# One fp32 product per attention step instead of three split ones, and score masks added in PSUM by VectorE

## The reference

```
s_c = q @ k_cmp - slope * d_c          p_c = masked_softmax(s_c, d_c >= 0)           o_c = p_c @ v_cmp
s_s = q @ k_selected - slope * d_s     p_s = masked_softmax(s_s, d_s >= 0)           o_s = p_s @ v_selected
s_w = q @ k_window - slope * d_w       p_w = masked_softmax(s_w, 0 <= d_w < 512)     o_w = p_w @ v_window
out = gate0 * o_c + gate1 * o_s + gate2 * o_w
```

## Time and profile before

| | |
|---|---|
| time, median of 3 runs | 1501.54 us (1500.02 to 1504.7) |
| profiled execution | 1494.26 us, span 1492.6 us |
| PE busy | 1435.1 us, 96% of the span |
| PEld, DVE, ACT, POOL busy | 1140.0, 736.6, 448.3, 123.4 us |
| chain that ended last | PE 87%, DVE 4%, issue 2%, POOL 2%, ACT 2% |
| granted clock of PE, 40 slices | 9999999799997999999999999999999999999998 |
| DMA | 67.61 MB, 45 GB/s over the span |

### The profile page before, as it was taken

One profiled execution on the slowest core, in us unless ns is written; L12 is line 12 of the kernel. 1 busy time (PEld: TensorE's weight loads), 2 busy tenths in 40 slices (PEclk: granted clock), 3 DMA queues, 4 the chain that ended last, 5 costly groups with the idle time before them and its releaser, 6 DMA issues.

```text
span 1492.6 us, 17479 instructions
## 1 busy us (share of the span) xinstructions
PE 1435.1 (96%) x6654; PEld 1140.0 (76%) x6654; DVE 736.6 (49%) x916; ACT 448.3 (30%) x635; POOL 123.4 (8%) x85
## 2 busy tenths in 40 slices
PE   7999999999897998989999999999999999999996
PEld 6788888876565765668888888888888888888884
DVE  6333511496665956655344435344443534444355
ACT  6211201404786047843132121212112121211212
POOL 0011000000111001110001000101000010100013
PEclk9999999799997999999999999999999999999998
DMA  5111120000000030011101111111111111111102
GB/s 207 53 57 56 33 89 33 9 1 4 1 1 6 1 116 1 1 57 57 56 29 57 43 57 57 42 42 56 42 42 56 56 42 42 56 42 42 56 0 112
DMA packets 19837, 67.61 MB, mean 45 GB/s; under 512 B 2216, under 2 KB 2984, under 8 KB 19624
## 3 DMA queue, kind: packets, MB, share of 16 engines
q1 hardware_dynamic: 19548, 66.03, 13.0%
q0 software_dynamic: 240, 0.93, 0.3%
HBM read 63.01 MB, written 4.19 MB: 45 GB/s over the span
## 4 chain that ended last, share of the span: by engine, by line
PE 87%; DVE 4%; issue 2%; POOL 2%; ACT 2%; DMA 1%; SPq 0%; DVEq 0%; POOLq 0%; ACTq 0%
PE PS L321 18%; PE PS L322 18%; PE PS L325 18%; PE PS L1303 5%; PE PS L1300 5%; PE PS L1299 5%; PE PS L1108 3%; PE PS L1109 2%; PE PS L1204 2%; PE PS L1206 1%; PE PS L1205 1%; PE PS L1185 1%; DVE nmax L824 1%; PE PS L1186 1%; PE PS L1090 1%
## 5 line engine op out<-in xcount | busy, mean ns | idle before, releaser
L321 PE MATMUL PS<-R,wh 128*128 128x512 f32 x1200 | 470.3, 392 | 13.1 <-DVE wl L313 11.2
L322 PE MATMUL PS<-R,wh 128*128 128x512 f32 x1200 | 468.2, 390 | 0.0
L325 PE MATMUL PS<-R,wl 128*128 128x512 f32 x1200 | 370.7, 390 | 0.0
L321 PEld LDWEIGHTS PS<-R,wh 128*128 128x128 f32 x1200 | 226.2, 188 | 61.2 <-DVE wl L313 11.7
L325 PEld LDWEIGHTS PS<-R,wl 128*128 128x128 f32 x1200 | 226.0, 188 | 47.3
L322 PEld LDWEIGHTS PS<-R,wh 128*128 128x128 f32 x1200 | 225.9, 188 | 47.4 <-issue 0.7
L306 ACT ACTIVATE wh<-raw 128x1024 fp32r<-128x1024 f32 x97 | 101.9, 1050 | 260.2 <-PE PS L1303 174.0
L961 DVE TENSOR_TENSOR F<-PS,F 128x1024 f32<-128x1024 f32 x80 | 97.8, 1223 | 86.6 <-PE PS L1303 86.6
L876 DVE TENSOR_TENSOR wl<-raw,wh 128x512 fp32r<-128x512 f32 x148 | 102.7, 696 | 59.1 <-ACT raw L605 57.1
L1300 PE MATMUL PS<-R,wh 128*128 128x512 f32 x320 | 124.5, 389 | 0.0
L1299 PE MATMUL PS<-R,wh 128*128 128x512 f32 x320 | 124.5, 389 | 0.0
(11 more groups left out here) (159 smaller groups left out, 1459.6 us busy)
## 6 DMA issues: line engine op xcount, KB each, us to landing
raw<-in_w_units SPq DMA_DIRECT2D x97, 512.0 KB, 3.4
F<-in_xT SPq DMA_DIRECT2D x16, 512.0 KB, 8.5
outT<-F SPq DMA_DIRECT2D x16, 256.0 KB, 2.2
F<-in_w_cmp SPq DMA_DIRECT2D x1, 2048.0 KB, 7.9
masks<-in_masks POOLq DMA_DIRECT2D x1, 448.0 KB, 4.9
R<-in_alibi_q POOLq DMA_DIRECT2D x2, 160.0 KB, 4.5
R<-R SPq DMA_DIRECT2D x4, 48.0 KB
R<-in_alibi_k POOLq DMA_DIRECT2D x1, 136.0 KB, 3.6
```

What stands on the lines that cost most here:

```text
L321: nc.tensor.matmul(out, w_h, hi(kt)[:, cols], start=first, stop=False)
L322: nc.tensor.matmul(out, w_h, lo(kt)[:, cols], start=False, stop=False)
L325: last = nc.tensor.matmul(out, w_l, hi(kt)[:, cols], start=False, stop=end)
```

## The change

- The exponential is taken once, in fp32, into `EB`. `V` is kept unsplit in fp32, in `PBm`. `values(s)` is a single fp32 product, V against `EB[s % 4]`.
- In the second pass the mask is no product any more: DVE adds it to the scores in PSUM (`mask_tile`), two steps ahead of its other work of a step, and ACT waits for it. The masks for the keys' side lie transposed in `masks` (diagonal and edge) and, for the compressed branch, in a new 512 KB table `CM` that POOL's queue loads ahead of the ALiBi rows. The first pass keeps its mask products. NEG becomes -2**100.
- `OT` moves from `PBm` to F1 slots 5 and 6. So SP loads the residual input for k = 2..7 where it did, and k = 0, 1 after the last `turn`. The copy of V ahead of its transposition is gone.
- The loop over the groups is written out on every engine, with constants in the waits.
- Weight units 24 to 26 wait for the last value product instead of the last subtraction, since `EB` lies in `raw`.

```diff
-NEG = -1e30
+NEG = -2.0 ** 100
...
+        def mask_of(s):
+            i, br, j = STEPS[s]
+            if br == 2:
+                return f32(CM[:, i * P:(i + 1) * P])
+            if j == i:
+                return masks[:, M_TILES:M_TILES + P]
+            return masks[:, M_TILES + P:M_TILES + 2 * P] if br == 1 and j == i - WT else None
...
-            with sp.Fori(0, KV) as g:
+            for g in range(KV):
...
-            for k in range(KT):
+            for k in range(2, KT):
                 sp.dma_start(F1[:, X1 + k, :], xT[k]).then_inc(x1_in, 16)
-            sp.wait_ge(pt_lo, KV * NS)
+            sp.wait_ge(pv_done, KV * NS)
             load(sp, 24, 0, 0, 0)
             load(sp, 25, 0, 0, 0)
             load(sp, 26, 0, 0, 0)
+            sp.wait_ge(ot_turned, KV * TT)
+            for k in range(2):
+                sp.dma_start(F1[:, X1 + k, :], xT[k]).then_inc(x1_in, 16)
...
             pool.dma_start(KB[DH:DH + AR + MR, :], alibi_k).then_inc(ak_in, 16)
-            with pool.Fori(0, KV) as g:
+            pool.dma_start(CM, cmp_masks_d).then_inc(cm_in, 16)
+            for g in range(KV):
...
-            with act.Fori(0, KV) as g:
+            for g in range(KV):
...
-                        nc.scalar.activation(PTH[s % 4], PS[:, s % 4, :], ACT.Exp).then_inc(pt_hi, 1)
-                        nc.scalar.activation(EB[s % 4], PS[:, s % 4, :], ACT.Exp).then_inc(e_ready, 1)
+                for s in range(NS):
+                    act.wait_ge(st_ready, NS * g + s + 1)
+                    if mask_of(s) is not None:
+                        act.wait_ge(masked, masked_upto(g, s))
+                    if s > 3:
+                        act.wait_ge(pv_done, NS * g + s - 3)
+                    nc.scalar.activation(EB[s % 4], PS[:, s % 4, :], ACT.Exp).then_inc(e_ready, 1)
+                    later(s)
...
+                def mask_tile(s):
+                    mask = mask_of(s)
+                    if mask is None:
+                        return
+                    dve.wait_ge(st_ready, NS * g + s + 1)
+                    scores = PS[:, s % 4, :].rearrange("p (h q) -> p h q", h=GROUP)
+                    nc.vector.tensor_tensor(scores, scores, mask.rearrange("p (o q) -> p o q", o=1)
+                                            .broadcast_to([P, GROUP, P]), ALU.add).then_inc(masked, 1)
...
+                mask_tile(0)
+                mask_tile(1)
                 for s in range(NS + 6):
-                    if s < NS:
-                        dve.wait_ge(e_ready, NS * g + s + 1)
-                        nc.vector.tensor_tensor(PTL[s % 4], EB[s % 4], f32(PTH[s % 4]), ALU.subtract).then_inc(pt_lo, 1)
+                    if s + 2 < NS:
+                        mask_tile(s + 2)
...
-                    nc.tensor.matmul(out, VH[:, n, 0:DH + 1], PTH[s % 4], start=first, stop=False)
-                    nc.tensor.matmul(out, VL[:, n, 0:DH + 1], PTH[s % 4], start=False, stop=False)
-                    nc.tensor.matmul(out, VH[:, n, 0:DH + 1], PTL[s % 4], start=False, stop=end).then_inc(pv_done, 1)
+                    nc.tensor.matmul(out, V[:, n, 0:DH + 1], EB[s % 4], start=first, stop=end).then_inc(pv_done, 1)
```

More of the change, by code:

```diff
@@ L76 @@
 NCON = 2 * P + TT
[L79 to L80 removed]
+M_ID, M_DIAG, M_EDGE, M_CMP = 0, P, 2 * P, 3 * P
+M_TILES = M_CMP + TT * CW
+NMASK = M_TILES + 2 * P
 class Steps:
@@ L189, in f32, with masked_upto @@
             return ap.bitcast(F32)
+        def mask_of(s):
[5 more added lines that the diff above has]
+            return masks[:, M_TILES + P:M_TILES + 2 * P] if br == 1 and j == i - WT else None
+        def masked_upto(g, s):
+            tiles = [n for n in range(NS) if mask_of(n) is not None]
+            return len(tiles) * g + sum(n <= s for n in tiles)
         consts_in, late_in, w1_in, ak_in = sem("consts_in"), sem("late_in"), sem("w1_in"), sem("ak_in")
-        masks_in, params_in = sem("masks_in"), sem("params_in")
+        masks_in, params_in, cm_in, masked = sem("masks_in"), sem("params_in"), sem("cm_in"), sem("masked")
         g_hi, g_lo, r_ready, conv_ready, tapr_ready = (sem("g_hi"), sem("g_lo"), sem("r_ready"), sem("conv_ready"),
@@ L593, in _, with later @@
                 act.wait_ge(vt_ready, g + 1)
[L594 to L595 removed]
+                nc.scalar.activation(V[:, 0:2 * TT, 0:DH].rearrange("p (b j) d -> p b j d", b=2),
+                                     pair(2).rearrange("p (j b d) -> p b j d", b=2, d=DH), ACT.Copy).then_inc(v_ready, 1)
                 act.wait_ge(kvc_ready, 2 * g + 2)
[L597 to L605 removed]
+                nc.scalar.activation(V[KCMP:KCMP + NCMP, 2 * TT, 0:DH], CMP_OUT[1][0:NCMP, 0:DH], ACT.Copy).then_inc(kc_hi, 1)
+                def later(s):
                     if s - 2 in ENDS and ENDS.index(s - 2) % 3 == 1:
@@ L614, in _ @@
                         act.wait_ge(o_ready, TT * g + i + 1)
-                        nc.scalar.activation(SQ_HEADS, F1[:, bass.ds(Q0 + 2 * g, 2), i * P:(i + 1) * P], ACT.Square,
-                                             accum_out=head_ss[:, bass.ds(TT * g + i, 1)]).then_inc(osq_ready, 1)
+                        nc.scalar.activation(SQ_HEADS, F1[:, Q0 + 2 * g:Q0 + 2 * g + 2, i * P:(i + 1) * P], ACT.Square,
+                                             accum_out=head_ss[:, TT * g + i:TT * g + i + 1]).then_inc(osq_ready, 1)
+                for s in range(NS):
[6 more added lines that the diff above has]
+                    later(s)
+                for s in range(NS, NS + 3):
+                    later(s)
                 act.wait_ge(pv_done, NS * g + NS)
@@ L791, in _ @@
             nc.vector.tensor_copy(posb[:, :], PS[:, 7, BANK // 2:BANK // 2 + 2]).then_inc(posb_ready, 1)
-            with dve.Fori(0, KV) as g:
-                steps.enter(g, KV, 2 * TT)
+            for g in range(KV):
                 for half in range(2):
@@ L885, in _ @@
                             part(STEP_OF_TURN.index(s - later))
-                steps.leave()
             dve.wait_ge(osq_ready, KV * TT)
@@ L1083, in _ @@
             pe.wait_ge(ak_in, 16)
-            pe.wait_ge(clear_ready, 5)
-            with pe.Fori(0, KV) as g:
+            pe.wait_ge(clear_ready, 4)
+            for g in range(KV):
                 def compressed_hidden(kv, src, pairs=range(CMP_BLOCK // 2)):
@@ L1181, in key_scores @@
                     flat = lambda q: q.rearrange("p h q -> p (h q)")
-                    mask = {0: M_DIAG if j == i else None,
-                            1: M_DIAG if j == i else M_EDGE if j == i - WT else None,
-                            2: M_CMP + i * P}[br]
                     nc.tensor.matmul(out, KA[:, cols], flat(QA[:, i, :, :]), start=True, stop=False)
                     last = nc.tensor.matmul(out, KB[0:DH + AR + MR, cols], flat(QB[0:DH + AR + MR, i, :, :]),
-                                            start=False, stop=mask is None)
-                    if mask is not None:
-                        last = nc.tensor.matmul(out, masks[:, mask:mask + P], masks[:, M_ID:M_ID + GROUP * P],
-                                                start=False, stop=True)
+                                            start=False, stop=True)
                     last.then_inc(st_ready, 1)
@@ L1458 @@
     first = lambda a: np.asarray(a)[0].reshape(16, P, P).transpose(1, 0, 2).reshape(P, 2, 1024)
-    consts, masks, aq, ak = _shape_constants()
+    consts, masks, cmp_masks, aq, ak = _shape_constants()
     arrays = {
@@ L1464 @@
         "w_cmp2": A(np.stack([np.asarray(w_ck2)[0], np.asarray(w_cv2)[0]], axis=1)),
-        "params": A(params), "consts": consts, "masks": masks, "alibi_q": A(aq), "alibi_k": ak,
+        "params": A(params), "consts": consts, "masks": masks, "cmp_masks": cmp_masks, "alibi_q": A(aq), "alibi_k": ak,
     }
```

84 lines of the change are left out of this document (33 added, 51 removed).

## The result

| | before | after |
|---|---|---|
| time, median | 1502.72 us (1500.02 to 1504.7, 4 runs) | 1489.21 us (1488.22 to 1493.21, 4 runs) |
| ratio | | 0.9917, 95% interval 0.9899 to 0.9935 |
| profiled execution | 1494.26 us, clock 0.981 | 1493.21 us, clock 0.978 |
| PE busy | 1435.1 us, 96% | 1449.6 us, 97% |
| DVE, ACT busy | 736.6, 448.3 us | 676.1, 381.5 us |

The change makes the kernel 12.5 us faster by the ratio. The two profiled executions say something else again: they differ by 1.05 us. That of before was shorter than each of its four timed runs, that of after the longest of its own. So the first lesson is to ask which execution a profile shows.

A forecast was written before the change was run, and what follows sets the result against it. PE was taken as the bound in the second pass, and its loop jump and lower clock as the cost between groups. Second passes +1.4 us and between groups -5.7 gave -4.3: 1497.2 us from a 1501.54 median, range 1491.5 to 1503.

The forecast's parts named there:

- the last of the sum: Whole kernel: -4.3 us, made against the profiled 1494.26 us, applied to the median 1501.54, 7.28 higher, giving 1497.2.
- Streaming: Second pass on PE: one fp32 product for three adds 24.7 us, masks leaving PE save 12.3; +12.4 us in all.
- Waits: Second pass: PE's waits shrink from 9.5 to 4.0 us per group, bounds 0 and 9.5; with streaming +1.4 us in all.
- 98.2 + 6.2 + 2.5: Second pass per group, us: old streaming with eight turnings, added streaming, and the tail after the last turning that stays.
- Between the groups: From group 0's last scaling to group 1's scores: writing the loop out removes PE's jump; -5.7 us, bounds 0 and -9.
- the first of the two cases: Between the groups: PE's clock falls all the same, near 464.1 us, during the compression; 5.0 us saved.
- a rival: Between the groups: the gap stays, or its gain returns as a wait for the ALiBi rows; 1502.9 us, chance 0.20.
- Edits at nothing: First-pass masks, V copy, mask table, weight units 24 to 26 and residual slots 0 and 1: each counted at 0 us.
- Clock kept, waits gone: Second-pass waits fall to 1.5 us per group and the clock stays up entering group 1: 1492.5 us, chance 0.20.
- Masks late: Second pass: DVE's mask additions sit behind scaling and bank copies, exposing 16 scalings, 15.5 us: 1512.7 us, chance 0.10.

The follow-up runs named there:

- after_again: The changed kernel itself, unchanged, timed and profiled again: 1489.57 us, ratio 0.9931 to the kernel before.
- before_filled: The kernel before plus ten unread matmuls per group where PE waits for the window copy at tile 3: 1497.99 us, ratio 0.9987.
- unroll_only: The kernel before with the loops over the groups written out on every engine, nothing else: 1493.28 us, ratio 0.9954.
- before_held: The kernel before plus unread matmuls in four PE waits per group (ALiBi rows, maxima, last scaling, tile 3): 1489.44 us, ratio 0.9932.
- fill_only_2: The changed kernel plus unread matmuls in three PE waits per group (maxima, last scaling, ALiBi rows): 1484.5 us, ratio 0.9884 to the kernel before.
- The square: Written-out loops, ratios to the kernel before: split products 0.9954 (masks on PE), 1.0076 (on DVE); one fp32 product 0.9976 (PE), 0.9931 (DVE).
- one_product: The changed kernel with its second-pass masks taken back to products on PE, single fp32 product kept: 1498.46 us, ratio 0.9976 to the kernel before.
- split_dve_masks: The kernel before with written-out loops and masks added by DVE, three split products kept: 1513.31 us, ratio 1.0076.
- pe_unrolled: The kernel before with the loop over the groups written out on PE alone: 1497.11 us, ratio 0.9961.
- loops_kept: The changed kernel with the group loops kept as loops and a copy of V ahead of its transposition: 1494.57 us, ratio 0.9964 to the kernel before.
- filled_all: The changed kernel plus earlier ALiBi load for group 1 and unread matmuls in three waits and among group-entry products: 1482.55 us, ratio 0.9878 to before.

## Why the prediction was wrong

**The step that failed** is the last of the sum: "a difference carries over: 1501.54 - 4.3 = 1497.2". The 4.3 us were made against an execution of 1494.26 us, which gave 1490.0. The profile of after_again, with the same entry of group 0 as that one, has 1489.15, so up to here the sum was nearly right. The 7.28 us added after that did not carry over: the changed kernel's median (1489.21) lies on its profile, not 7 us above it. They were the kernel before's own loss. Its profiled execution had a clock of 0.981, its usual one has 0.976 to 0.977; at 1.24 to 1.5 us per 0.001 that is 5 to 7.5 us.

Shown: the time of before follows its clock; matmuls that nobody reads, whose only use is to keep PE busy in its waits, gain 10.6 us in the kernel before and 5 in the changed one; and with these in both kernels the difference falls to 4.9 us (6.6 by the means). Not shown: where the usual execution of before loses more clock than that of after. The wait for the window copy at tile 3 is one such place, with up to 4.0 us per pass, and in the changed kernel it is down to 0.4 us; but with this wait filled before_filled recovered only 2 of the 10.6 us. unroll_only has the wait too, and none of its six runs is above 1494.5 us. The entry of group 0 moves executions by up to 4.6 us in either kernel. Nor is it known what decides in a single execution whether the clock falls behind a wait of 2.5 us.

Point by point, by the prediction's own terms:

- **Streaming, +12.4 us.** Right in its parts: 0.86 us for the fp32 product, 0.23 for a score product, 1.32 per step (0.86 + 2 x 0.23).
- **Waits, 9.5 to 4.0 us per group.** Mis-sized, by 1.3 us per group. With the clock at its upper level in both, the pass is 110.2 us before and 109.6 after [before_held, fill_only_2], -0.6 per group where +0.7 was forecast. 98.2 + 6.2 + 2.5 leave 2.7 us of waits instead of 4.0. In the two groups that is -1.1 instead of +1.4, within its bounds of -6.6 and +12.4. The square shows how: the dearer product, which takes longer than the chain behind it needs, hides the waits it would otherwise meet (110.2 to 115.0 us with masks on PE, 4.8 us for 148 / 2 x 0.167 = 12.4 of streaming), and on top of that the masks' 6.15 us of streaming give 3.6 (115.0 to 111.4), or 5.4 against the pass with fillers (109.6).
- **Between the groups, -5.7 us.** The size was right (-5.6 and -5.1 in the two profiles), the make-up only in part. The gap was PE's jump, 4.0 us. The clock did fall, as in the first of the two cases, which had 5.0 us. In the first profile the bound behind it is the load of the ALiBi rows after POOL's sums, which I had only named in a rival. The gain beyond the gap goes roughly with how long after PE's start the clock falls: 1.9 us in after and 1.8 in one_product (stage of 7.32 and 7.76 us), 1.0 in after_again (7.90), 0.5 in split_dve_masks (8.43), and before the start in unroll_only and pe_unrolled (8.85, as before). What sets that is open. The Trainium skill's rule on sequential prefetch (Runtime: NRT & Kernel Launch, section Instruction fetch mechanics) says that a taken branch to a page that isn't held has to fetch it first. The trace agrees as far as it goes: 0.05 us in straight code, 3.62 to 4.05 with the loop.
- **Edits at nothing.** All held. Everything behind the last scaling takes 841.58 us, against 841.91. PE waits nowhere for the residual input. The mask table delays nothing: in after_again the first score product of group 0 starts at 288.80 us, against 289.67 before.
- **Rivals.** "Clock kept, waits gone" came nearest in time (1492.5) and had 0.20. It was priced by waits at 1.5 us per group and a clock that stays up at the entry of group 1. The waits did go, the clock at the entry did not stay. That the time came out near this rival is luck: about half of the gain is clock that the kernel before loses in executions that no profile shows, and the rival had it elsewhere. "Masks late" was wrong here. Something like it happens in split_dve_masks, where DVE has the subtraction as well: +12 us in the pass of group 0, by waits for the subtraction (10.3 us) and the clock.

## What to carry to other kernels

A profile is one execution. Before a difference is added to a median, compare the mean clock of the profiled execution with the clocks of the timed runs; where they differ, part of the median hangs on the clock, and it need not come back in another kernel. Before two profiles are subtracted, look for a stage ahead of the change that differs between them. Two edits on one path are priced together: here each alone made group 0's second pass longer, by 4.8 us (a product that is dearer but leaves an engine free) and 11.9 (a job given to that engine), and both together by 1.2. PE's waits of 1 to 3 us were worth filling with matmuls that nobody reads into a free bank: 5 us in the changed kernel, 10.6 in the kernel before.

## What the runs showed of the hardware

- The jump back to the head of PE's loop over the groups costs 3.6 to 4.1 us (loops_kept 3.62, before_filled 4.10), and 0.05 where the loop is written out. In the other engines' lists it is hidden here (pe_unrolled, where only PE's is written out, has 0.05 as well).
- The same wait of about 2.6 us in PE's stream was followed by full clock in one execution (before) and by 6.8 us at the lower level in another (pe_unrolled).
- The time of the kernel before falls by 1.24 us for each 0.001 of mean granted clock (82 runs, 0.969 to 0.981).
- At the entry of group 0 of the changed kernel PE is listed busy for 12.05 us, and then 7.54 of 8.83, at a granted clock of 0.64 and then 0.50, which is its lower level (1.2 GHz):

```profile
272.00:284.05 12.05, 12.05 (x74) 12.05 (x72) 3.13 (x5) 6.55 (x7) 3.00 (x7) 0.64 0.28 69
284.05:292.88 8.83, 7.54 (x36) 7.20 (x36) 5.40 (x8) 2.40 (x5) 0.00 (x0) 0.50 0.00 0
```

With fillers of 512 columns among its products (filled_all) the same two stages take 10.32 and 6.80 us, fillers included, with no time at the lower level.
